# Inverting the delta rule's triangular matrix in 32x32 blocks instead of 64x64 ones

## The reference, cut to what matters

```python
def gated_delta_chunked(q, k, v, g, beta):
    ...
    strict = jnp.tril(jnp.ones((c, c), bool), -1)
    decay = jnp.exp(jnp.where(causal, G[..., :, None] - G[..., None, :], -jnp.inf))
    kb = k * beta[..., None]
    m = jnp.where(strict, jnp.einsum('bhnrd,bhnsd->bhnrs', kb, k) * decay, 0.0)
    t_mat = m + jnp.eye(c, dtype=m.dtype)
    w = lax.linalg.triangular_solve(t_mat, kb * jnp.exp(G)[..., None],
                                    left_side=True, lower=True, unit_diagonal=True)
    u = lax.linalg.triangular_solve(t_mat, v * beta[..., None],
                                    left_side=True, lower=True, unit_diagonal=True)
    ...
```

## Time and profile before

| | |
|---|---|
| median of 3 runs | 1038.84 us (1038.66 to 1039.63) |
| the profiled execution, its own time | 1039.35 us |
| its span, first to last instruction | 1037.6 us |
| PE busy | 1015.5 us, 98% of the span |
| DVE busy | 841.6 us, 81% |
| ACT busy | 627.8 us, 61% |
| granted TensorE clock | 0.998 of full speed |
| DMA | 174.35 MB, mean 168 GB/s |

### The profile page before, as it was taken

The page is one execution under the profiler, slowest core; times in us unless marked ns, Lnnn a source line. Parts: engine busy times, 40 slices in busy tenths (PEclk is TensorE's granted clock), DMA queues, the critical chain, the costliest instruction groups (busy, mean ns, idle before and its releaser), DMA issues.

```text
span 1037.6 us, 20750 instructions
## 1 busy us (share of the span) xinstructions
PE 1015.5 (98%) x8313; PEld 946.6 (91%) x8313; DVE 841.6 (81%) x1183; ACT 627.8 (61%) x858; POOL 5.9 (1%) x16
## 2 busy tenths in 40 slices
PE   7999999999999999999999999999999999999996
PEld 6999889998999999899999999989999999999985
DVE  6966797699988878877999888779775899988876
ACT  6764566566665654556666556667576566555556
POOL 0000000000000000000000000000000000000000
PEclk9999999999999999999999999999999999999999
DMA  9432223455655545564566455344434355655531
GB/s 328 169 123 83 83 84 123 149 191 196 210 192 182 192 163 167 191 223 150 187 213 218 168 197 196 128 163 163 163 123 142 132 193 195 210 196 181 190 123 41
DMA packets 26290, 174.35 MB, mean 168 GB/s; under 512 B 3133, under 2 KB 3413, under 8 KB 6000
## 3 DMA queue, kind: packets, MB, share of 16 engines
q1 hardware_dynamic: 25520, 171.17, 47.7%
q0 software_dynamic: 704, 2.23, 0.7%
HBM read 172.33 MB, written 1.06 MB: 167 GB/s over the span
## 4 chain that ended last, share of the span: by engine, by line
PE 84%; DVE 8%; ACT 5%; DMA 2%; issue 1%; SPq 0%; DVEq 0%; ACTq 0%
PE PS L539 70%; PE PS L490 13%; DVE w_lo L2141 2%; ACT w_hi L1415 1%; DMA arena<-masks_in 1%; DVE x L2674 1%; DVE h_store L2154 1%; DVE arena L2668 1%; DMA raw<-weights 1%; DVE arena L2670 0%; PE PS L1325 0%; ACT h_store L1432 0%; DVE h_store L2984 0%; DVE arena L2270 0%; DVE arena L2521 0%
## 5 line engine op out<-in xcount | busy, mean ns | idle before, releaser
L539 PE MATMUL PS<-h_store,w_hi 128*128 128x512 f32 (+1 forms) x1808 | 482.8, 341 | 10.4 <-DVE w_lo L2185 7.3
L2141 DVE TENSOR_TENSOR w_lo<-raw,w_hi 128x2048 fp32r<-128x2048 f32 x156 | 357.0, 2290 | 56.9 <-ACT w_hi L1415 51.8
L539 PE MATMUL PS<-h_store,w_lo 128*128 128x256 f32 (+1 forms) x1384 | 374.1, 282 | 0.0
L539 PEld LDWEIGHTS PS<-h_store,w_hi 128*128 128x128 f32 x1808 | 305.5, 188 | 53.4 <-DVE w_lo L2185 7.3
L1415 ACT ACTIVATE w_hi<-raw 128x2048 fp32r<-128x2048 f32 x157 | 299.6, 1910 | 80.4 <-PE PS L539 66.6
L539 PEld LDWEIGHTS PS<-h_store,w_lo 128*128 128x128 f32 (+1 forms) x1384 | 256.5, 189 | 0.3
L539 PE MATMUL PS<-act_hi,w_hi 128*128 128x256 f32 x704 | 196.5, 281 | 0.1
L539 PE MATMUL PS<-act_hi,w_lo 128*128 128x256 f32 x704 | 195.3, 279 | 0.0
L539 PE MATMUL PS<-act_lo,w_hi 128*128 128x256 f32 x704 | 192.5, 279 | 0.0
L539 PEld LDWEIGHTS PS<-act_hi,w_hi 128*128 128x128 f32 x704 | 132.3, 188 | 2.5 <-issue 1.6
L539 PEld LDWEIGHTS PS<-act_hi,w_lo 128*128 128x128 f32 x704 | 132.4, 188 | 0.2 <-issue 0.2
(11 more groups left out here) (336 smaller groups left out, 1122.2 us busy)
## 6 DMA issues: line engine op xcount, KB each, us to landing
raw<-weights SPq DMA_DIRECT2D x157, 1024.0 KB, 4.9
arena<-masks_in SPq DMA_DIRECT2D x1, 1472.0 KB, 12.2
x<-x_in SPq DMA_DIRECT2D x4, 256.0 KB, 4.2
raw<-weights SPq DMA_DIRECT2D x4, 256.0 KB, 5.5
raw<-weights SPq DMA_DIRECT2D x2, 512.0 KB, 9.1
arena<-bias_by_distance POOLq DMA_DIRECT2D x1, 1024.0 KB, 7.7
result<-arena SPq DMA_DIRECT2D x4, 256.0 KB, 2.1
arena<-p_in POOLq DMA_DIRECT2D x2, 256.0 KB, 4.3
```

The costliest lines, as they stand in the source:

```text
L539: return pe.matmul(o, lhs, rhs, start=start, stop=stop, skip_group_check=True)
L2141: tt(w_lo[:, slot, :], raw[:, slot, :], w_hi[:, slot, :].bitcast(F), ALU.subtract).then_inc(lo_ready, 1)
```

## The change

The inverse is built only up to blocks of 32x32, and for all of them at once: the 128 rows are four quarters of 32, which are the four 32x32 diagonal blocks of the two chunks. Operands are packed as 128x8x32 (8 units of 32 columns), and a product is 32 matmuls of 32x32x32, each on a diagonal quarter of the array (rows 32q to 32q+31 in, PSUM partitions 32q to 32q+31 out), all in one PSUM bank. DVE and ACT then handle a product with one instruction of 128x256 where there were two of 64x512. Four levels (0 to 3) are like that. The fifth joins the blocks of a chunk: with A and D the inverses of the even and odd diagonal blocks and B the block below the diagonal, `gdn_cx(4)` computes B A on 16 matmuls from the even rows to the odd partitions, and `gdn_xcx(4)` brings (B A)^T D^T to the even partitions and a copy of D^T (by the identity) to the odd ones, 32 matmuls. DVE writes both halves of `inv_full` (128x8x64), from which `gdn_solve` works as before. `gdn_turn_m` now makes the transposes of the 32x32 diagonal blocks (32 matmuls into bank 0) and of the blocks below them (16 matmuls from the odd rows to the even partitions of bank 1). Eight masks of 32 columns are new, as two more of the 128-column masks: the mask DMA carries 25 x 128 columns instead of 23 x 128. The weight ring, the projections between the steps, and everything after `gdn_solve` stay.

```diff
+         "blocks0", "blocks1")
-        mt_gd = place([P, 8, CHUNK])
-        c_t = place([P, 8, CHUNK])
+        mt_full = place([P, 8, CHUNK])
+        c_full = place([P, 8, CHUNK])
         ngd_tri = place([P, 8, CHUNK])
-        inv, inv_t, y_gd = dec, dec_t, m_gd
+        HALF = CHUNK // 2
+        two_blocks = lambda v: [b.rearrange("p u n -> p (u n)").rearrange("p (u n) -> p u n", n=HALF) for b in (v[:, 0:4, :], v[:, 4:8, :])]
+        inv, inv_t = two_blocks(dec)
+        mt_gd, mt_across = two_blocks(mt_full)
+        c_t, y_gd = two_blocks(c_full)
+        inv_full = dec_t
...
@@ -905,43 +927,60 @@
 
             def gdn_turn_m():
                 pe.wait_ge(sem("m_ready"), 1)
-                turn_chunks(0, m_gd).then_inc(once("m_turned")[0], 1)
-
-            def chunk_products(bank, lhs, rhs):
-
                 for u in range(8):
-                    for c in range(2):
-                        r = rows_of_chunk(c)
-                        last = mm(chunk_bank(bank, u, c), lhs[r, u, :], rhs[r, u, :])
+                    for q, r in enumerate(QUARTERS):
+                        mm(block_at(0, u, r), m_gd[r, u, HALF * (q % 2):HALF * (q % 2 + 1)], ident[r, r])
+                for u in range(8):
+                    for even, odd in (QUARTERS[0:2], QUARTERS[2:4]):
+                        last = mm(block_at(1, u, even), m_gd[odd, u, 0:HALF], ident[odd, odd])
+                last.then_inc(once("m_turned")[0], 1)
+
+            def block_products(bank, lhs, rhs):
+
+                for u in range(8):
+                    for r in QUARTERS:
+                        last = mm(block_at(bank, u, r), lhs[r, u, :], rhs[r, u, :])
                 return last
 
             def gdn_cx(lv):
 
-                pe.wait_ge(sem("inv_ready"), 2 * lv + 1)
-                pe.wait_ge(sem("ct_ready"), lv + 1)
-                chunk_products(2, c_t, inv).then_inc(sem("cx"), 1)
+                pe.wait_ge(sem("inv_ready"), lv + 1)
+                if lv < 4:
+                    pe.wait_ge(sem("ct_ready"), lv + 1)
+                    block_products(2, c_t, inv).then_inc(sem("cx"), 1)
+                    return
+                for u in range(8):
+                    for even, odd in (QUARTERS[0:2], QUARTERS[2:4]):
+                        last = mm(block_at(2, u, odd), mt_across[even, u, :], inv[even, u, :])
+                last.then_inc(sem("cx"), 1)
 
             def gdn_xcx(lv):
-                pe.wait_ge(sem("cx_copied"), 2 * lv + 2)
-                pe.wait_ge(sem("inv_t_ready"), 2 * lv + 1)
+                pe.wait_ge(sem("cx_copied"), lv + 1)
+                pe.wait_ge(sem("inv_t_ready"), lv + 1)
                 if lv < 4:
-                    chunk_products(6, inv_t, y_gd).then_inc(sem("xcx"), 1)
-                chunk_products(0, y_gd, inv_t).then_inc(sem("xcx"), 1)
+                    block_products(6, inv_t, y_gd).then_inc(sem("xcx"), 1)
+                    block_products(0, y_gd, inv_t).then_inc(sem("xcx"), 1)
+                    return
+                for u in range(8):
+                    for even, odd in (QUARTERS[0:2], QUARTERS[2:4]):
+                        mm(block_at(0, u, even), y_gd[odd, u, :], inv_t[odd, u, :])
+                        last = mm(block_at(0, u, odd), ident[odd, odd], inv_t[odd, u, :])
+                last.then_inc(sem("xcx"), 1)
 
...
@@ -1618,13 +1657,14 @@
 
             def gdn_turn_m():
                 act.wait_ge(*once("m_turned"))
-                chunk_copy(mt_gd, 0, 0)
-                chunk_copy(mt_gd, 0, 1).then_inc(once("mt_ready")[0], 1)
+                act.activation(flat(mt_gd), PS[:, 0, 0:8 * HALF], ACT.Copy)
+                for even in QUARTERS[0:3:2]:
+                    ins = act.activation(flat(mt_across[even]), PS[even, 1, 0:8 * HALF], ACT.Copy)
+                ins.then_inc(once("mt_ready")[0], 1)
 
             def gdn_cx(lv):
                 act.wait_ge(sem("cx"), lv + 1)
-                for c in range(2):
-                    chunk_copy(y_gd, 2, c).then_inc(sem("cx_copied"), 1)
+                act.activation(flat(y_gd), PS[:, 2, 0:8 * HALF], ACT.Copy).then_inc(sem("cx_copied"), 1)
...
@@ -2327,33 +2367,39 @@
 
                 dve.wait_ge(sem("m_ready"), 1)
                 dve.wait_ge(*once("decay_turned"))
-                link(tt(inv, m_gd, units(packed(6), 8), ALU.mult))
-                tt(inv, units(packed(-1), 8), inv, ALU.subtract).then_inc(sem("inv_ready"), 1)
+                mark(tt(inv, m_gd[:, :, 0:HALF], units(block_mask("pair_even"), 8), ALU.mult))
+                mark(tt(inv_t, m_gd[:, :, HALF:CHUNK], units(block_mask("pair_odd"), 8), ALU.mult))
+                settle()
+                link(tt(inv, units(block_mask("eye"), 8), inv, ALU.subtract))
+                tt(inv, inv, inv_t, ALU.subtract).then_inc(sem("inv_ready"), 1)
 
             def gdn_first_turned():
                 dve.wait_ge(*once("mt_ready"))
-                tt(c_t, mt_gd, units(packed(1), 8), ALU.mult).then_inc(sem("ct_ready"), 1)
+                tt(c_t, mt_gd, units(block_mask(1), 8), ALU.mult).then_inc(sem("ct_ready"), 1)
                 gdn_a_qk()
                 dve.wait_ge(sem("qk_gram_read"), 1)
-                link(tt(inv_t, mt_gd, units(packed(0), 8), ALU.mult))
-                tt(inv_t, units(packed(-1), 8), inv_t, ALU.subtract).then_inc(sem("inv_t_ready"), 1)
+                dve.wait_ge(sem("inv_ready"), 1)
+                link(tt(inv_t, mt_gd, units(block_mask(0), 8), ALU.mult))
+                tt(inv_t, units(block_mask("eye"), 8), inv_t, ALU.subtract).then_inc(sem("inv_t_ready"), 1)
 
             def gdn_next_block(lv):
 
                 dve.wait_ge(sem("cx"), lv + 1)
-                tt(c_t, mt_gd, units(packed(lv + 2), 8), ALU.mult).then_inc(sem("ct_ready"), 1)
+                tt(c_t, mt_gd, units(block_mask(lv + 2), 8), ALU.mult).then_inc(sem("ct_ready"), 1)
 
             def gdn_xcx(lv):
                 flat = lambda v: v.rearrange("p u n -> p (u n)")
                 if lv < 4:
-                    dve.wait_ge(sem("xcx"), 2 * lv + 1)
-                    for c in range(2):
-                        r = rows_of_chunk(c)
-                        tt(flat(inv[r]), flat(inv[r]), PS[r, 6 + c, :], ALU.subtract).then_inc(sem("inv_ready"), 1)
-                dve.wait_ge(sem("xcx"), 2 * lv + 2 if lv < 4 else 9)
-                for c in range(2):
-                    r = rows_of_chunk(c)
-                    tt(flat(inv_t[r]), flat(inv_t[r]), PS[r, c, :], ALU.subtract).then_inc(sem("inv_t_ready"), 1)
+                    for k, (x_gd, ready) in enumerate(((inv, sem("inv_ready")), (inv_t, sem("inv_t_ready")))):
+                        dve.wait_ge(sem("xcx"), 2 * lv + k + 1)
+                        tt(flat(x_gd), flat(x_gd), PS[:, 6 - 6 * k, 0:8 * HALF], ALU.subtract).then_inc(ready, 1)
+                    return
+                dve.wait_ge(sem("inv_t_ready"), 5)
+                mark(ts(inv_full[:, :, 0:HALF], inv_t, half_sign("even"), None, ALU.mult))
+                dve.wait_ge(sem("xcx"), 9)
+                mark(ts(inv_full[:, :, HALF:CHUNK], PS[:, 0, 0:8 * HALF].rearrange("p (u n) -> p u n", n=HALF),
+                        half_sign("minus_even_plus_odd"), None, ALU.mult))
+                signal(sem("inv_t_ready"), 1)
...
@@ -2581,9 +2627,9 @@
             gdn_first_turned()
             block_lo(9)
             for lv in range(5):
-                if lv < 4:
+                if lv < 3:
                     gdn_next_block(lv)
-                else:
+                if lv == 4:
                     gla_queries_and_keys()
                     block_lo(11)
                 if lv in (1, 2):
+    pack.append(np.concatenate([i_in < 32, np.where(i_in < 32, -1, 1), np.zeros((P, CHUNK - 2))], axis=1))
+    i_blk, j_blk = r % 32, c[:, 0:32]
+    pair = (i_blk // 2 == j_blk // 2) & (j_blk < i_blk)
+    blocks = [i_blk == j_blk, pair & (i_in < 32), pair & (i_in >= 32)]
+    for lv in range(5):
+        b = 1 << lv
+        blocks.append((i_blk // (2 * b) == j_blk // (2 * b)) & (i_blk % (2 * b) < b) & (j_blk % (2 * b) >= b))
+    for j in range(2):
+        one[f"blocks{j}"] = np.concatenate(blocks[4 * j:4 * j + 4], axis=1)
```

More of the change, by code:

```diff
@@ L59 @@
 MASKS = ("e1", "e2", "e4", "e8", "e16", "e32", "e64", "after", "tri", "ones", "tri_again",
-         "fox_add", "gdn_add", "eye", "blk_tri", "blk_after", "ind0", "ind1", "same", "packed0", "packed1", "packed2", "packed3")
+         "fox_add", "gdn_add", "eye", "blk_tri", "blk_after", "ind0", "ind1", "same", "packed0", "packed1", "packed2", "packed3",
+         "blocks0", "blocks1")
 MASK = {n: i for i, n in enumerate(MASKS)}
@@ L309, in packed, with block_mask, half_sign @@
             return masks.rearrange("p m n -> p (m n)")[:, at:at + CHUNK]
+        def block_mask(name):
+            at = MASK["blocks0"] * P + ("eye", "pair_even", "pair_odd", 0, 1, 2, 3, 4).index(name) * HALF
+            return masks.rearrange("p m n -> p (m n)")[:, at:at + HALF]
+        def half_sign(name):
```

(18 more changed lines are left out.)

## The result

The changed kernel takes 1041.59 us (median of 9 runs, 1040.02 to 1043.17), the kernel before 1039.38 on the same chip (9 runs): ratio 1.0020, interval 1.0012 to 1.0028. The forecast was 1033.5, its range 1032.0 to 1037.0.

What follows compares the result with a forecast made beforehand. TensorE's stream was taken to bound the kernel. Shorter products save 6.0 us, the mask load costs 0.3, so 5.7 saved from the profiled 1039.35; stated as 1033.5 against the median of 1038.84, range 1032.0 to 1037.0.

Steps and rivals of the forecast that it cites:

- What bounds the kernel: From transposed decay to solve, TensorE is always busy (39.65 us), so shorter products save time one for one if operands are ready.
- The step: In the small products, four records on four quarters start together every 31 ns, against 58 ns for two before.
- one bank and one writer: Rival: a PSUM bank takes one row group's records at a time in the products, 16.1 us slower, 1054.9; chance 0.08.
- two quarters at a time: Rival: the array runs only two quarters together, a step of four takes 62 ns, time 1040.0; chance 0.04.
- What is late next: In the levels, ACT's copies (0.4 us) and DVE's subtractions (0.41 each) stay hidden, 1.6 us of slack where tightest; cost nothing.
- The masks: At the kernel's start, the mask load grows by 131 KB and costs 0.3 us, all exposed.
- the stream of instructions: Rival: 480 matmuls instead of 240 make instruction supply the products' bound; 1039.1 or a half-way gain; chances 0.05 and 0.12.
- part-way gain: Half-way cases: waits for instruction loading inside the denser products leave a gain of 1.8 to 3.3 us; chance 0.12.
- unchanged time: Instruction-bound case: products keep their time, gdn_turn_m's cost and gdn_cx(4)'s saving are 0.5 each, masks remain: 1039.1; chance 0.05.
- the sum itself: TensorE's savings: 5.2 us in levels 0 to 3, twice 0.43 in level 4, less 0.06 in gdn_turn_m: 6.0.

Runs made afterwards that it cites:

- the run with half products: Changed kernel with each product of levels 0 to 3 cut to units 0 to 3 (16 of 32 matmuls): 1032.04 us, ratio 0.9925.
- the first burst: Kernel before with 256 more 32x32x32 matmuls on the diagonal quarters ahead of level 0's first product, output overwritten: 1056.6 us.
- 64 records more: Changed kernel with 32 more 32x32x32 matmuls ahead of the decays' turn, results overwritten: 1047.71 us, ratio 1.0075.
- both bursts: Kernel before with extra 32x32x32 matmuls ahead of level 0's first product, 256 of them or twice as many: 1056.6 and 1068.13 us.
- its shifts: Changed kernel with 64 or 128 more records of 32x32x32 matmuls ahead of the decays' turn, results overwritten: 1047.71 and 1047.59 us.

## Why the prediction was wrong, by its steps

- **What bounds the kernel.** Right that TensorE's stream sets the end. Wrong that a shorter product is "time saved one for one, as long as the operands of the next are ready": the instructions must be ready too.
- **The step.** 31 ns predicted for four records. Eight steps more take 0.68 - 0.38 = 0.30 us in the run with half products, 37 ns; sixteen more take 1.24 - 0.68 = 0.56, 35 ns. A product became 0.40 us shorter, a pair 0.77: 1.17 a level, where 3 x 0.43 = 1.29 was said. Level 4's two gave 0.46 and 0.40 for 0.43 each. gdn_turn_m costs 0.27 beside its stall, not 0.06. In sum 4.7 + 0.86 - 0.27 = 5.3 us instead of 6.0.
- **The banks.** The rival of one bank and one writer (1054.9) and the one of two quarters at a time (1040.0) are refuted by the same rows: four tiles write one bank in steps of 35 ns, where they asked for 124 and 62. The Trainium skill's "Gotcha 1: PSUM Pressure" (TensorEngine Tiling (Array Packing)) does not hold here, for tiles that write different quarters of the partitions; the measurement decides.
- **What is late next.** Right: no wait of TensorE in the stage names ACT or DVE; ACT's copy takes 0.38 us, DVE's pair of subtractions 0.98.
- **The masks.** 0.3 us predicted, 0.2 measured with an uncertainty of 0.9; the step is neither confirmed nor wrong.
- **The step that failed: the stream of instructions.** I had named it, with the 16 KB packets, but gave a part-way gain 0.12, "unchanged time" 0.05 and a loss nothing, and the sum itself priced it at zero: "no idle time of TensorE between gdn_turn_m and the solve". There were 5.2 us. What I left out was a sum that the earlier trace rows allowed in part: 480 records more are 3.75 packets, all inside 36 us. With the borders found later it comes close: a level has 192 + 24 = 216 records. Where it stalls in every packet, the ends of the stalls are 79.86 - 76.19, 83.70 - 79.86 and 87.53 - 83.70 = 3.67 to 3.84 us apart, so a level takes 216 / 128 x 3.8 = 6.4 us; the four took (96.38 - 70.31) / 4 = 6.5. Before, it took 6.32 (68.47 to 74.79), with 120 records that needed one packet in 6.7 us. The products got shorter; the levels got as long as their packets.
- **From 5.3 us saved to 1.2 lost.** That is 6.5 us in the stage: 5.2 idle, the rest the restarts: a product cut in two by a stall takes 0.2 us longer (0.24 + 0.66 in place of 0.68 at 75.47), and six cuts make 1.3. The 0.7 to 1.0 us that the whole kernel lost beyond the stage's 1.2 stay open; they are about what two profiled executions differ by, as the second profile of the changed kernel reaches gdn_turn_m 0.4 us before the first. Open too is why a packet sometimes starts only 6 us after the last one, as in the first burst and, with 64 records more, ahead of the stall of 1.93 us.

## What to carry to other kernels

Before splitting matmuls into smaller ones, count records against time: here 128 float32 records needed a packet of instructions, one came per 3.5 to 3.8 us when TensorE waited for it, and any stretch denser than that (27 to 30 ns a record) ran at the loading's pace, with stalls at fixed record counts. A chain that never leaves a busy engine says that its work bounds the end, not that less work of more instructions would be faster. Keep tiles of one shape together, and when the bounding engine shows "issue" pieces, look at instructions first: count the records between them.

## What was not expected of the hardware

- Long stalls for instructions went with a lower granted clock: it fell to 0.50 for 6.8 us behind one of 1.93 us and within one of 3.94, and within the second stall of both bursts, while those up to 1.14 us in the changed kernel and its shifts left it at 1.00. Work then takes up to twice as long (2.86 us for 1.6).
- The stalls repeat from run to run on the same matmul, though their length varies (0.49 and 1.04 us at the same one).
- A change between 32x32 and 64x64 tiles within a product costs 0.14 us, as much as four steps of 35 ns; one between 32x32 and the whole array 0.15. Both are estimates, worked out above.
- With a single projection matmul after every 16 records the clock was 0.50 for 44 us in the profile, in which TensorE was never idle.
